# Reordering of projection pieces among recurrence levels, a split rotary step and later key stores in a diffusion-backbone step on one Trainium2 core

## The reference, cut to what matters

```
z = einsum('bld,de->ble', h, w_in)                 # 3584 columns
hq, hff, hfb, hi, hg, aq, ak, av, hy = _split_cols(z)
o_hg, s_fin = _hgrn_mixer(hq, hff, hfb, hi, hg, lb, s0, norm_g)   # gated linear recurrence, both directions
qh, kh = _axial_rope(qh), _axial_rope(kh)           # latent tokens only
rot: xa * cos(ang) + concatenate([-x2, x1]) * sin(ang)
o_da = _diff_attention(qh, keys, vals, lam)         # 4 heads, two softmax maps each
x = x + g1 * (concat(o_hg, o_da, o_hy) @ w_out)
x = x + g2 * _ec_ffn(...)                           # 16 experts
```

## Time and profile before

| | |
|---|---|
| median of three runs | 4094.68 us |
| profiled execution, its time | 4091.86 us |
| its span | 4090.1 us |
| TensorE matmul busy | 3777.7 us, 92% |
| TensorE weight loads busy | 3031.7 us, 74% |
| VectorE busy | 1606.4 us, 39% |
| ScalarE busy | 1157.8 us, 28% |
| GpSimd busy | 182.8 us, 4% |
| mean granted TensorE clock | 0.96 of full speed |

### The profile page before, as it was taken

How to read it: one execution, slowest core, us unless ns; L and a number is a source line. 1 busy time by engine, 2 the same in 40 slices (tenths; PEclk the granted TensorE clock), 3 DMA queues, 4 the chain that set the end, 5 groups by cost and what they waited for, 6 DMA issues and landing times. The chain is left out here.

```text
span 4090.1 us, 55577 instructions
## 1 busy us (share of the span) xinstructions
PE 3777.7 (92%) x23486; PEld 3031.7 (74%) x23486; DVE 1606.4 (39%) x2860; ACT 1157.8 (28%) x2938; POOL 182.8 (4%) x112
## 2 busy tenths in 40 slices
PE   8899998997969999999889999989879699999996
PEld 3466875666439999999735778656664499999995
DVE  4238723878351111111152487238783511111112
ACT  3452212884121111111144322138731211111112
POOL 0000001000000000000000000110000000000000
PEclk9999999998979999999999999999989799999998
DMA  7411021002347777778482110210122477877774
GB/s 281 148 52 47 30 81 71 1 1 108 114 160 257 273 268 272 268 274 279 173 301 87 49 44 30 88 61 1 47 88 99 154 280 278 279 271 272 279 279 169
DMA packets 318559, 645.83 MB, mean 158 GB/s; under 512 B 19742, under 2 KB 57246, under 8 KB 317544
## 3 DMA queue, kind: packets, MB, share of 16 engines
q1 hardware_dynamic: 305064, 594.04, 40.2%
q0 software_dynamic: 9216, 33.56, 3.5%
q10 hardware_dynamic: 4032, 14.68, 0.9%
HBM read 580.36 MB, written 61.88 MB: 157 GB/s over the span
## 5 line engine op out<-in xcount | busy, mean ns | idle before, releaser
L2183 PE MATMUL ps<-arena 128*128 128x144 f32 x8192 | 1017.1, 287 | 6.7 <-DVE arena L2401 6.7
L2183 PEld LDWEIGHTS ps<-arena 128*128 128x128 f32 x8192 | 1010.2, 191 | 14.6 <-DVE arena L2401 14.6
L291 PE MATMUL ps<-arena 128*128 128x384 f32 x1920 | 628.6, 488 | 4.0 <-PEq L89 4.0
L291 PEld LDWEIGHTS ps<-arena 128*128 128x128 f32 x1920 | 364.3, 191 | 251.7 <-issue 7.8
L2207 PE MATMUL ps<-arena 128*128 128x144 f32 x4096 | 507.1, 286 | 0.0
L2207 PEld LDWEIGHTS ps<-arena 128*128 128x128 f32 x4096 | 503.6, 190 | 0.0
L2412 DVE TENSOR_TENSOR arena<-arena,ps 128x144 f32<-128x144 f32 x256 | 77.9, 304 | 922.2 <-ACT arena L2289 922.2
L2289 ACT ACTIVATE arena<-ps 128x144 f32<-128x144 f32 x256 | 74.3, 290 | 988.6 <-PE ps L2183 988.6
L433 ACT ACTIVATE arena<-ps 128x384 f32<-128x384 f32 (+1 forms) x192 | 86.1, 448 | 693.7 <-PE ps L291 462.0
L2401 DVE TENSOR_SCALAR arena<-ps,mod 128x128 f32<-128x128 f32 x248 | 84.5, 403 | 448.5 <-PE ps L2161 448.5
L288 PE MATMUL ps<-arena 128*128 128x256 f32 x1152 | 257.0, 381 | 0.0
(11 more groups left out here) (351 smaller groups left out, 3505.1 us busy)
## 6 DMA issues: line engine op xcount, KB each, us to landing
arena<-in_w_gate SPq DMA_DIRECT2D x64, 2048.0 KB, 8.0
arena<-in_w_up SPq DMA_DIRECT2D x64, 2048.0 KB, 14.1
arena<-in_w_down SPq DMA_DIRECT2D x64, 2048.0 KB, 12.4
arena<-in_w_mod SPq DMA_DIRECT2D x24, 2048.0 KB, 15.5
arena<-in_w_in SPq DMA_DIRECT2D x28, 1024.0 KB, 5.1
arena<-in_dft_units SPq DMA_DIRECT2D x26, 512.0 KB, 10.8
arena<-x_rows SPq DMA_DIRECT2D x21, 512.0 KB, 6.6
filter_spectra<-arena SPq DMA_DIRECT2D x8, 1024.0 KB
```

Source lines behind the costliest of these rows:

```text
L291: last = nc.tensor.matmul(m.ps[:, at:at + TC], m.Wr[:, slot % 2, k, jj * P:(jj + 1) * P], m.hT[:, k, q * TC:(q + 1) * TC], start=(k == 0), ...
L2183: last = nc.tensor.matmul(m.ps[:, at:at + CAP], m.wbuf[:, 2 * h + which, k, q * P:(q + 1) * P], m.xe[:, e % 2, k, :], start=(k == 0), stop ...
```

## The change

Four edits. TensorE issues four pieces, not three, between the state updates and level 0, and so one fewer among the levels. The levels without a piece behind them are 2, 5, 8, 11, 14, 19 and 27, where they were 3, 7, 11, 19, 23 and 27. ScalarE's evictions follow the same lists. The rotation of the last key block is done in two parts: tokens 0 to 767 when the second of its three pieces is taken, and tokens 768 to 1023 when the third is. The context keys are stored by SP at the start of the attention stage, behind its loads, and are waited for at that stage's end. `m.kout` moves from column 17408 to 2304 of the arena, into the region of the stage's input.

```diff
-    AT_LEVELS = FIRST_HY + 10
-    with_piece = [n for n in range(NS) if n % 4 != 3 or n in (15, 31)]
+    AT_LEVELS = FIRST_HY + 11
+    with_piece = [n for n in range(NS) if n not in (2, 5, 8, 11, 14, 19, 27)]
...
+    ROPE = [(i, 0, LAT, end_of(5 + i // 2, i % 2)) for i in range(7)]
+    ROPE += [(7, 0, 2 * TC, end_of(8) - 1), (7, 2 * TC, LAT, end_of(8))]
...
             sp.wait_ge(s["s_stored"], 128)
-            sp.wait_ge(s["k_taken"], 3)
-            for h in range(HEADS):
-                sp.dma_start(m.o["k"][l, h].rearrange("m t d -> t m d"),
-                             m.kout[:, h].rearrange("p (m d) -> p m d", d=DQ)).then_inc(s["kv_stored"], 16)
-            sp.wait_ge(s["kv_stored"], 16 * (HEADS + 1))
+            sp.wait_ge(s["kv_stored"], 16)
...
-            for i in range(8):
-                pool.wait_ge(s["shuffled"], i + 1)
-                x = m.aqk[:, i, 0:LAT]
-                nc.gpsimd.tensor_tensor(x, x, m.cos[:, :], ALU.mult).then_inc(s["kept"], 1)
+            for n, (i, a, b, _) in enumerate(ROPE):
+                pool.wait_ge(s["shuffled"], n + 1)
+                x = m.aqk[:, i, a:b]
+                nc.gpsimd.tensor_tensor(x, x, m.cos[:, a:b], ALU.mult).then_inc(s["kept"], 1)
...
             state_updates()
-            for _ in range(3):
+            for _ in range(4):
                 piece()
...
-            for i in range(8):
-                dve.wait_ge(s["taken"], end_of(5 + i // 2, i % 2))
-                x = m.aqk[:, i, 0:LAT]
-                r = m.rot[:, i % 2]
+            for n, (i, a, b, ready) in enumerate(ROPE):
+                dve.wait_ge(s["taken"], ready)
+                x = m.aqk[:, i, a:b]
+                r = m.rot[:, n % 2, a:b]
...
     (attention, sync engine)
             sp.dma_start(m.sub_gain[:, :], m.d["diff_subln_col"][l]).then_inc(s["z_loaded2"], 16)
+            for h in range(HEADS):
+                sp.dma_start(m.o["k"][l, h].rearrange("m t d -> t m d"),
+                             m.kout[:, h].rearrange("p (m d) -> p m d", d=DQ)).then_inc(s["keys_stored"], 16)
             sp.wait_ge(s["spectra_loaded"], 32)
+            sp.wait_ge(s["keys_stored"], 16 * HEADS)
...
-        m.kout = view(17408, HEADS, P)
+        m.kout = view(2304, HEADS, P)
```

More of the change, by code:

```diff
@@ L737, in _ @@
             t = Count(s["turned"])
-            for i in range(8):
-                dve.wait_ge(s["taken"], end_of(5 + i // 2, i % 2))
-                x = m.aqk[:, i, 0:LAT]
-                r = m.rot[:, i % 2]
+            for n, (i, a, b, ready) in enumerate(ROPE):
+                dve.wait_ge(s["taken"], ready)
+                x = m.aqk[:, i, a:b]
+                r = m.rot[:, n % 2, a:b]
                 nc.vector.stream_shuffle(r, x, [(k + 16) % 32 for k in range(32)]).then_inc(s["shuffled"], 1)
-                dve.wait_ge(s["shuffled"], i + 1)
-                t.then_wait(dve, nc.vector.tensor_tensor(r, r, m.sin[:, :], ALU.mult))
-                dve.wait_ge(s["kept"], i + 1)
+                dve.wait_ge(s["shuffled"], n + 1)
+                t.then_wait(dve, nc.vector.tensor_tensor(r, r, m.sin[:, a:b], ALU.mult))
+                dve.wait_ge(s["kept"], n + 1)
                 nc.vector.tensor_tensor(x, x, r, ALU.add).then_inc(s["roped"], 1)
@@ L785, in attention @@
     SHORT_AT = {4: (0, 0), 8: (0, 1), 12: (0, 2), 16: (1, 0), 20: (1, 1), 24: (1, 2)}
-    with stage(nc, m, "spectra_loaded", "z_loaded0", "z_loaded1", "z_loaded2", "centred", "tapped", "scores0", "scores1", "scores2", "step", "peak", "probs0", "probs1", "probs2", "ratio", "combined",
+    with stage(nc, m, "spectra_loaded", "keys_stored", "z_loaded0", "z_loaded1", "z_loaded2", "centred", "tapped", "scores0", "scores1", "scores2", "step", "peak", "probs0", "probs1", "probs2", "ratio", "combined",
                "turned", "taken", "valued", "row_out") as (block, s):
```

## The result

The changed kernel takes 4062.68 us (median of four runs, 4060.77 to 4066.53) against 4091.99 us of the kernel before (four runs, 4089.23 to 4098.86): a ratio of 0.9927, 95% interval 0.9915 to 0.994. That is 29.3 us less, where 25.8 were forecast. The median of the kernel before has a fourth run in it here and lies 2.7 us under the 4094.68 us on which the forecast of 4069 us stands. The span fell from 4090.1 to 4062.4 us, 27.7 us.

What follows compares the result with a forecast made beforehand. TensorE bounds the kernel, its matmuls filling 92% of the span. Levels 17.6, stage's end 6.9 and attention's start 1.3 sum to 25.8 us, giving 4069 us against the median 4094.68; range 4061 to 4081.

Steps and rivals of the forecast that it cites:

- Edit 1: Before level 0: the extra piece runs inside TensorE's wait, 5.16 us gained a layer, 1.1 us of idle left.
- a choice between bounds: Level 0's clock term: full clock behind the short hole, 1.92 us in layer 0, 1.68 in layer 1; lower bound 0.
- Edit 2: Among the levels: level 24's wait goes, 3.83 us plus slow matmuls of 2.58 or 1.79, less 4.20 of new waits.
- the four waits that take its place: New TensorE waits: level 9, 1.10 us; recurrent_out, 1.55; level 24, 0.45; level 28, 1.10; 4.20 us a layer.
- The first rival: Levels: short holes cost clock too, 9.7 us in layer 0 and 7.1 in layer 1; ends at 4086; chance 0.12.
- The rule of the Trainium skill: TensorE: frequent micro-idles between groups of matmuls can make the clock swing; by it the sum would be the 4086 us case.
- The rival in which VectorE becomes the bound: Levels 2, 5, 8, 11 and 14 each wait as level 24 did, 30 us a layer; ends at 4123; chance 0.03.
- Both terms together: Levels, extra piece and new list summed: 9.3 us in layer 0, 8.3 in layer 1, together 17.6 us.
- Edits 3 and 4: Stage's end: split rotation and late stores let attention start at 691.75, not 695.18; 3.4 us a layer, 6.9 in two.
- GpSimd's quarter: Stage's end: GpSimd's work on the last 256 tokens, taken as 0.85 us; bounds 0.85 and the whole 3.38.
- The rival without a gain at the end: Stage's end: something unseen holds the barrier to 695, so only 17.6 us comes; 4077; chance 0.10.
- attention's start: First 12 scores run quicker behind a 1.6 us hole: 0 to 1.65 us a layer, 0.65 taken, 1.3 in all.

Runs made afterwards that it cites:

- the three kernels with the old levels: Kernel before with split rotation and late key stores, 4084.42 us; with late stores alone, 4093.16 us; with split rotation alone, 4087.19 us.
- the kernel without them: Changed kernel with levels 1, 5, 9, 13, 16, 29 and 30 without a piece; single time 4059.73 us beside 4092.56 us of the kernel before.
- the one with two pieces ahead: Changed kernel with one more piece ahead of level 0, levels 0, 3, 6, 9, 13, 16, 29, 30 without; median 7.4 us under the changed kernel.

## Why the prediction was right, and where not

**Edit 1.** The piece runs inside level 0's wait: the start of level 0 behind the state updates is the same to 0.03 us, the idle 1.17 us (forecast 1.1), the level 2.25 us. That the short hole would bring no half clock was a choice between bounds, and it was the right end. How much half clock the kernel before had there was partly chance: of the 8.85 us in layer 0, 1.2 to 1.5 are there only against that one profile (see the three kernels with the old levels). Against those the change is worth 7.4 to 7.7 us.

**Edit 2.** Level 24's wait went, and the four waits that take its place stand where the count put them, 4.15 us for 4.20. The first rival (short holes cost clock too) is out: no wait of 0.2 to 1.5 us in any of these kernels' levels brought slow matmuls. The rule of the Trainium skill weighed there (TensorE: Matmul & The Clock Gate, "A second HAM failure mode: psum-queue depth-cycling") does not show at this rate of holes. From level 0 to level 28 of layer 0, some 160 us, there are six such waits at a granted clock of 1.00. The rival in which VectorE becomes the bound is out in the same way; two more kernels with other lists lost all the new small waits, so VectorE had the time. Both terms together were forecast at 9.3 and 8.3 us and came to 8.85 and 7.87. The missing 0.4 us a layer were not in the sum: a level behind any wait takes 2.25 us in place of 2.17, recurrent_out's first four matmuls 0.71 in place of 0.61, and there are five such restarts now. They went together with the waits in the kernel without them.

**Edits 3 and 4.** Forecast 3.4 us a layer, measured 3.45. That each edit alone would leave the other's wait was argued from three end times, one of which the trace only bounded; it is now shown (0.40 and 0.01 us). GpSimd's quarter took 0.97 us, near the low bound of 0.85 and far from 3.38, and the barrier opened 0.34 us behind ScalarE. The rival without a gain at the end is out.

**The mis-sized term** is attention's start: "0 to 1.65 us a layer. I take 0.65". The mechanism was right (the half clock behind the hole), the size not. The 12 scores take 2.42 us, not 2.99: I had scaled from eight matmuls of 512 columns, but the last four have 256. So 2.22 and 1.40 us came off them. TensorE's first scores in layer 1 and VectorE's first three maxima in layer 0, kernel before:

```profile
2722.20 3.82 PE L812 MATMUL ps<-arena 64*128 64x512 f32 x12 [5.07 <-PEq L89]
```

```profile
697.34 1.22 DVE L880 TENSOR_REDUCE arena<-ps 128x2 f32<-128x1024 f32 x1 [2.92 <-PE ps L812]
699.04 1.82 DVE L880 TENSOR_REDUCE arena<-ps 128x2 f32<-128x1024 f32 x2 [0.48 <-PE ps L812]
```

The maxima of the kernel after, in layer 0, have no gap between them:

```profile
684.56 2.95 DVE L883 TENSOR_REDUCE arena<-ps 128x2 f32<-128x1024 f32 x3 [2.60 <-PE ps L815]
```

In the profiled pair the whole stage gained 1.77 and 2.79 us, 4.6 us where 1.3 was forecast. Other profiles with the short hole gained less, down to a loss of 0.24 us. The mean of the six profiles with it and no filler (both of the changed kernel, the end's edits alone, the three with other lists) is 0.7 and 1.7 us under the kernel before, that of the six with the long hole 1.15 and 0.15 over it. So the short hole is worth about 1.9 us a layer, with a scatter of the same size. What of the first scores' gain survives to the end of attention in a given run stays open.

The total: 16.7 + 6.9 + 4.6 us make 28.2, less 0.5 elsewhere, the 27.7 of the span. The medians' 29.3 differs from it by 1.6 us, less than the 5.8 us over which the four runs of the changed kernel spread. Part of the agreement is luck: 3.3 us too little at attention's start stand against 0.9 too much in the levels, and the profile after happened to have the largest attention gain of layer 0 among those with the short hole. The median of 4062.68 us is 6.3 under the 4069 forecast and only 1.7 above the range's lower end; 2.7 of the 6.3 come from the median before. The range's lower end was not worked out: the recorded bounds leave only 2.0 us under the forecast, at attention's start, and not "about 4".

## What to carry to other kernels

When two waits on different engines end within half a microsecond of each other before a barrier, neither is worth much alone (here 0.40 and 0.01 us of 3.45): list every engine's last end, and price the pair. To place filler work between steps of a two-engine pipeline, add up the slower engine's instructions from its last idle moment against the faster one's. Here that count gave each new wait to 0.1 us before it was built, and then a list without them. Short holes (here up to 1.6 us) cost their own length and 0.08 us of a slower restart; those of 4.67 us and more also cost clock behind them every time, and useless products in one saved it.

## What the runs showed of the hardware

A wait of 3.65 to 3.67 us on TensorE, between the same matmuls at level 24, was followed by 4.18 us, 2.86, 2.97 or 2.25 us for the same level. Over the five kernels that have this wait (3.65 to 3.68 us), both layers, the level took 4.18 us once, 2.86 to 3.09 seven times and 2.25 twice. So a hole of that length does not always cost clock, and two profiles can differ by 2.5 us there.

The largest scatter lies in a part that no kernel here touched, from the end of layer 0's attention to layer 1's state updates. It took 5.1 us less in the second profile of the changed kernel than in the kernel before, 5.2 in the end's edits alone, 5.4 in the rotation alone, 4.7 in the one with two pieces ahead, and lay within 0.5 us of the kernel before in the other eight. Most of it falls in the stage ahead of layer 1's projections. Both profiles of the changed kernel, the first and the second, by stretch:

```profile
2100.00:2170.00 70.00, 54.14 (x254) 28.17 (x253) 34.13 (x98) 29.32 (x68) 5.93 (x3) 0.80 0.67 239
```

```profile
2100.00:2170.00 70.00, 52.52 (x265) 27.70 (x264) 34.14 (x98) 31.66 (x71) 5.93 (x3) 0.90 0.67 238
```

The granted clock is 0.80 in the first and 0.90 in the second. In the same stretch it is 0.88 to 0.90 in the other three with the quicker course, and 0.80 to 0.83 in the kernel before and the other seven. TensorE has three waits of 3.3 to 3.5 us there in every profile, each before eight transposes. First profile of the changed kernel:

```profile
2117.94 1.94 PE L1150 MATMUL ps<-ident,arena 128*128 128x128 f32 x8 [3.40 <-DVE arena L1387]
...
2132.04 1.94 PE L1150 MATMUL ps<-ident,arena 128*128 128x128 f32 x8 [3.45 <-DVE arena L1387]
...
2142.65 1.94 PE L1150 MATMUL ps<-ident,arena 128*128 128x128 f32 x8 [3.47 <-DVE arena L1387]
```

Second profile:

```profile
2118.60 1.06 PE L1150 MATMUL ps<-ident,arena 128*128 128x128 f32 x8 [3.40 <-DVE arena L1387]
...
2132.39 1.94 PE L1150 MATMUL ps<-ident,arena 128*128 128x128 f32 x8 [3.47 <-DVE arena L1387]
...
2142.78 1.07 PE L1150 MATMUL ps<-ident,arena 128*128 128x128 f32 x8 [3.47 <-DVE arena L1387]
```

So a hole of this length, too, cost clock behind it one time and not the other. The transposes behind the third wait took 1.06 or 1.07 us in the four profiles with the quicker course, and 1.94 us, like those behind the other two, in all nine others. From 2113 to 2150 us the second profile gains 3.1 of the 4.9 us by which it is quicker than the first.

The transposes and the quicker course go together in all 13 profiles, but no kernel here changed these waits, so this is not put to a test. Some 5 us is also the gap between the two groups of runs of the end's edits alone, and the profiled one, of the lower group, has the quicker course. That the course makes the groups is not shown, since the other runs have no trace. A change of 5 us in this kernel is read from stretches of the trace and not from medians.

Issuing four stores of 64 KB took SP 1.92 us with idle queues at the stage's end, and 9.48 us behind 5.8 MB of loads.
